# Two attention turns merged: a score bank's read takes over the minimum of the piece in front, and the first stages' order changes

## The reference

```python
u = _rms(h, g_attn_pre)
q_da, k_da, v_da, cq, ckv, kr = jnp.split(u @ w_in, IN_SPLITS, axis=-1)
y_da = _diff_attention(...)   # 4 heads, two components of 64 each, values 128
y_mla = _mla(...)             # 4 heads, 128 + 64 rotary, values 128
h = h + _rms(jnp.concatenate([y_da, y_mla], -1) @ w_o, g_attn_post)
f = jnp.square(jax.nn.relu(_rms(h, g_mlp_pre) @ w_ff1)) @ w_ff2
h = h + _rms(f, g_mlp_post)
```

```python
s1 = (q1 @ k1) * scale + bias     # bias: -slope * distance, or -1e30 where masked
s2 = (q2 @ k2) * scale + bias
a = softmax(s1) - lam * softmax(s2)      # differential attention
p = softmax((q @ k) * scale + bias)      # latent attention, bias 0 or -1e30
```

## Time and profile before

| | |
|---|---|
| device time, median of 3 runs | 2669.18 us (2667.22 to 2671.14) |
| device time of the profiled execution | 2672.47 us |
| its span | 2670.7 us |
| TensorE busy | 2581.2 us, 97% |
| VectorE busy | 1629.5 us, 61% |
| ScalarE busy | 1212.4 us, 45% |
| POOL busy | 326.4 us, 12% |
| granted TensorE clock, mean | 0.99 |

### The profile page before, as it was taken

The page is one execution under the profiler, slowest core; times in us unless marked ns, Lnnn a source line. Parts: engine busy times, 40 slices in busy tenths (PEclk is TensorE's granted clock), DMA queues, the critical chain, the costliest instruction groups (busy, mean ns, idle before and its releaser), DMA issues.

```text
span 2670.7 us, 35310 instructions
## 1 busy us (share of the span) xinstructions
PE 2581.2 (97%) x12220; PEld 2119.1 (79%) x12220; DVE 1629.5 (61%) x3488; ACT 1212.4 (45%) x2177; POOL 326.4 (12%) x303
## 2 busy tenths in 40 slices
PE   8999999899998999999999999999999999999998
PEld 7997687666666888877877888878887887878786
DVE  6213303889996766664457777767767565564665
ACT  6112312577775555554454333533335353443554
POOL 1011001222221222220000000000000001111133
PEclk9999999899999999999999999999999999999999
DMA  6323356724533011016576677656645265666787
GB/s 224 128 102 105 103 166 206 194 62 110 126 133 91 29 37 48 25 51 194 175 243 205 206 240 218 217 168 215 214 135 195 104 225 103 157 171 155 184 174 137
DMA packets 331515, 398.85 MB, mean 149 GB/s; under 512 B 23488, under 2 KB 237744, under 8 KB 323024
## 3 DMA queue, kind: packets, MB, share of 16 engines
q1 hardware_dynamic: 313776, 364.68, 43.6%
q0 software_dynamic: 17568, 31.99, 8.3%
HBM read 240.13 MB, written 156.48 MB: 149 GB/s over the span
## 4 chain that ended last, share of the span: by engine, by line
PE 61%; DVE 3%; ACT 2%; DMA 1%; issue 1%; SPq 1%; POOL 0%; DVEq 0%; ACTq 0%; POOLq 0%
PE ff_ps_x L3143 25%; PE ff_ps_m L3143 13%; PE ff_ps_z L3143 6%; PE ml_ps_s L2026 6%; PE ff_ps_m L1586 4%; PE ml_ps_o L2055 4%; PE ml_ps_t L2039 2%; DMA ml_v_raw<-scr_yT 1%; DVE ff_mv_lo_p L2998 1%; DMA ff_pieces<-scr_acc 0%; PE ff_ps_r L2586 0%; PE mo_ps_t L2603 0%; ACT ff_mv_hi_p L2880 0%; SPq L2213 0%; DVE ff_pieces L2316 0%
## 5 line engine op out<-in xcount | busy, mean ns | idle before, releaser
L3143 PE MATMUL ff_ps_x<-ff_mv_hi_p,ff_st_hi_p 128*128 128x512 f32 x764 | 299.6, 392 | 11.4 <-DVE ff_mv_lo_p L2998 11.4
L3143 PE MATMUL ff_ps_x<-ff_mv_hi_p,ff_st_lo_p 128*128 128x512 f32 x764 | 299.1, 392 | 0.0
L3143 PE MATMUL ff_ps_x<-ff_mv_lo_p,ff_st_hi_p 128*128 128x512 f32 x764 | 298.9, 391 | 0.0
L2026 PE MATMUL ml_ps_s<-wide,ml_qs 128*128 128x416 f32 (+14 forms) x880 | 197.9, 359 | 2.9 <-PEq L137 2.7
L2993 DVE TENSOR_TENSOR ff_st_lo_p<-ff_ps_m,ff_st_hi_p 128x512 fp32r<-128x512 f32 x190 | 130.7, 688 | 104.0 <-ACT ff_st_hi_p L2870 104.0
L2837 POOL DMA_DIRECT2D scr_acc<-ff_pieces x64 | 55.4, 871 | 1030.7 <-DVE ff_pieces L3017 951.4
L3143 PEld LDWEIGHTS ff_ps_x<-ff_mv_hi_p,ff_st_hi_p 128*128 128x128 f32 x764 | 144.3, 189 | 43.5 <-issue 13.6
L2887 ACT ACTIVATE ff_u<-ff_ps_x 128x512 f32<-128x512 f32 x128 | 76.6, 599 | 215.7 <-PE ff_ps_x L3143 215.7
L3143 PEld LDWEIGHTS ff_ps_x<-ff_mv_hi_p,ff_st_lo_p 128*128 128x128 f32 x764 | 144.5, 189 | 30.2
L3143 PEld LDWEIGHTS ff_ps_x<-ff_mv_lo_p,ff_st_hi_p 128*128 128x128 f32 x764 | 144.6, 189 | 29.9
L2026 PEld LDWEIGHTS ml_ps_s<-wide,ml_qs 128*128 128x128 f32 x880 | 152.5, 193 | 18.8 <-issue 7.4
(11 more groups left out here) (298 smaller groups left out, 6375.0 us busy)
## 6 DMA issues: line engine op xcount, KB each, us to landing
st_raw<-in_w_ff SPq DMA_DIRECT2D x64, 512.0 KB, 6.1
scr_hid<-ff_pieces SPq DMA_DIRECT2D x128, 256.0 KB, 2.6
st_raw<-scr_hid SPq DMA_DIRECT2D x64, 512.0 KB, 5.0
ring<-in_w_ff SPq DMA_DIRECT2D x28, 1024.0 KB, 7.8
scr_t<-ring SPq DMA_DIRECT2D x24, 1024.0 KB, 6.4
ring<-scr_t SPq DMA_DIRECT2D x21, 1024.0 KB, 7.9
scr_acc<-ff_pieces POOLq DMA_DIRECT2D x64, 256.0 KB, 4.0
ring<-scr_u SPq DMA_DIRECT2D x13, 1024.0 KB, 8.3
```

What stands on the lines that cost most here:

```text
L2026: m = pe.matmul(ps_s[n % NSB][:, 0:w], q, k, start=j == 0, stop=j == len(pairs) - 1)
L3143: m = pe.matmul(bank[:, :], w[kind][:, k], a[kind][:, k], start=start and k == 0 and i == 0, stop=stop and k == KH - 1 and i == 2, skip_gr ...
```

## The change

Four groups of edits:

1. **First stages.** The second place for a split `cv_proj` weight lies over `in_proj`'s memory in such a way that it is free early; three of the four quarters, in the order 0, 2, 3, 1 (`CV_FIRST`), are split before `in_proj`'s last `high` and `low`, and the first product reads the quarters in that order. At the start the x tiles 4 and 5 are loaded before the second weight tile. POOL's gains in `in_proj` and in the second half of `cv_proj` become eight tensor_scalar operations of one eighth each, and the splits wait for the eighths that they need. SP loads `trig` for tile n + 2 directly behind the latent's store. VectorE's order at the end of the first half of `cv_proj` puts splits ahead of the normalising of the last two tiles.
2. **Both attentions.** The chunk read has scale -scale and takes the minimum, and its starting scalar is the result of the chunk before it (`lowest[..., nth - 1]`) instead of a constant. So `lowest` of the last chunk is the row's. There is no L1448 or L1948 any more; exp waits for `scores_read` of the last chunk and has scale -1. A chunk with a predecessor waits for `scores_read` of it, ahead of the hold.
3. **Memory.** `mx`, `nmax`, `nmax_all` give way to `lowest`.
4. **Squared-ReLU part.** For n = 0 the sum `c11` is added right behind step `p3` instead of behind `p7`.

```diff
             def gain(u):
-                pool.tensor_tensor(w_raw[:, u], w_raw[:, u], g_col[:, :].unsqueeze(2).broadcast_to([P, KD, P]),
-                                   ALU.mult).then_inc(w_gained, 1)
+                for k in range(KD):
+                    pool.tensor_scalar(w_raw[:, u, k], w_raw[:, u, k], g_col[:, k:k + 1], 1.0, ALU.mult, ALU.mult).then_inc(w_gained, 1)
...
             act.wait_ge(cv_gained, 1)
-            act.activation(quarter_of([w_hi], 0), cv_w[:, 0:KD // 4], ACT.Copy).then_inc(shared.w_hi_ready, 1)
+            for q in CV_FIRST[0:3]:
+                act.activation(quarter_of([w_hi, shared.w_hi_second], q), cv_w[:, KD // 4 * q:KD // 4 * (q + 1)], ACT.Copy).then_inc(shared.w_hi_ready, 1)
             high(NM - 1)
...
+CV_FIRST = (0, 2, 3, 1)
...
                 sp.dma_start(scr.latent[r0:r0 + rows, :], cn[0:rows, n % 2, QR:QR + KVR]).then_inc(latent_stored[n % 2], 16)
+                if n + 2 < N:
+                    load_trig(n + 2)
                 sp.wait_ge(lo_ready, n + 1)
                 for src, dst in ((o_hi, scr.c_hi), (o_lo, scr.c_lo)):
                     sp.dma_start(dst[:, :, r0:r0 + rows], f32(src[:, n % 2]).rearrange("p (f t) -> p f t", f=4)[:, :, 0:rows]).then_inc(stored[n % 2], 16)
-                if n + 2 < N:
-                    load_trig(n + 2)
...
             pool.wait_ge(w_loaded, 16 * len(CV_COLS[1]))
-            pool.tensor_tensor(cv_w[:, :, :], cv_w[:, :, :], g_col[:, :].unsqueeze(2).broadcast_to([P, KD, W]), ALU.mult).then_inc(w_gained, 1)
+            for k in range(KD):
+                pool.tensor_scalar(cv_w[:, k], cv_w[:, k], g_col[:, k:k + 1], 1.0, ALU.mult, ALU.mult).then_inc(w_gained, 1)
...
-            for n in range(N - 1):
+            for n in range(N - 2):
                 normalise(n)
                 if n:
                     low(n - 1, pt[(n - 1) % 2])
-            for g in range(NP, 2 * NP - 1):
+            split(NP)
+            normalise(N - 2)
+            for g in (NP + 1, NP + 2):
                 split(g)
+            low(N - 3, pt[(N - 3) % 2])
+            split(2 * NP - 1)
             normalise(N - 1)
-            split(2 * NP - 1)
             low(N - 2, pt[(N - 2) % 2])
             low(N - 1, pt[(N - 1) % 2])
...
             def exp(h, i, c, u, **at):
-                act.wait_ge(max_ready, NT * COMPS * h + COMPS * i + c + 1)
-                act.activation(comp_row(i, c, u), comp_row(i, c, u), ACT.Exp, bias=nmax[:, i % 2, c:c + 1], scale=scale,
+                n = last_chunk[i, c]
+                nth = nth_of(n)
+
+                act.wait_ge(scores_read, NCH * h + n + 1)
+                act.activation(comp_row(i, c, u), comp_row(i, c, u), ACT.Exp, bias=lowest[:, i % 2, c, nth:nth + 1], scale=-1.0,
                                accum_out=total[:, i % 2, c:c + 1]).then_inc(exp_ready, 1)
...
+                if nth:
+
+                    dve.wait_ge(scores_read, NCH * h + n)
 
                 hold(dve, scores_ready, NCH * h + n + 1)
                 dve.tensor_tensor_reduce(out=comp_row(i, c, u)[:, k0:k0 + w], in0=ps_s[n % NSB][:, 0:w],
-                                         in1=bias[u][:, b0:b0 + w], scale=1.0, scalar=LOWEST,
-                                         op0=ALU.add, op1=ALU.max,
-                                         accum_out=mx[:, i % 2, c, nth:nth + 1]).then_inc(scores_read, 1)
-                if k0 + w == META + P * (i + 1):
-                    dve.wait_ge(scores_read, NCH * h + n + 1)
-
-                    dve.tensor_scalar(nmax_all[:, 0:nth + 1], mx[:, i % 2, c, 0:nth + 1], -scale, None, ALU.mult, ALU.min,
-                                      accum_out=nmax[:, i % 2, c:c + 1]).then_inc(max_ready, 1)
+                                         in1=bias[u][:, b0:b0 + w], scale=-scale, scalar=lowest[:, i % 2, c, nth - 1:nth] if nth else -LOWEST,
+                                         op0=ALU.add, op1=ALU.min,
+                                         accum_out=lowest[:, i % 2, c, nth:nth + 1]).then_inc(scores_read, 1)
...
                 then("p3", n)
+                if n == 0:
+                    dve.wait_ge(product_done, done("p2", 0))
+                    add("c11", 0, ps_z, s1, c11_made)
                 hidden("c12", n, c12_made)
```

## The result

The changed kernel takes 2686.48 us (median of 4, 2685.11 to 2688.76), the one before 2669.43 (4 runs): ratio 1.0064, 95% interval 1.0049 to 1.008. It is slower by 17 us; the forecast was 10 slower.

A forecast was written before the change was run, and what follows sets the result against it. TensorE was taken as the bound, VectorE in rows 12 to 15 of each differential-attention head. From the 2669.2 us median, 14.5 us less in front and rest and about 25 more in the differential attention gave 2679 us, range 2655 to 2692.

The forecast's parts named there:

- The price of a dependent chunk: Differential attention: accumulator read 0.085, wait before a hold 0.145, pointer 0.06; 0.29 us when adjacent, 0.21 behind a reciprocal.
- how much reaches the end in rows 8 to 11: Differential attention: VectorE gets +3.4 us a head, mostly in its present pauses, so +1.2 (0.3 to 3) arrives.
- (a): Start: gain cut in 8 lets VectorE in between, x tiles load earlier; 1.5 us less (0 to 2.2).
- (b): First latent product: TensorE's wait for the second weight quarter goes, as three quarters are split earlier; 1.4 us less.
- (c): Latent stage: POOL's long block cut and trig load issued earlier remove TensorE's waits behind o_hi; 7 of 7.2 us.
- (d): Second half of the latent stage: splits ahead of the two last normalises remove two waits; 2.6 us less.
- (e): Squared-ReLU part: moving the c11 add ahead removes TensorE's wait for ScalarE's s1; 1.8 us less.
- (f): Latent attention: dependent chunks cost 0 because VectorE has a third of its time free; last row's chain 0.25 us shorter.
- 1, the cheap wait: Differential attention: wait and nop pass together, a dependent chunk costs 0.18 us; +7, net -7, 2662 us; chance 0.24.
- 2, the free wait: Differential attention: the wait costs nothing, only the pointer's 0.06 us a chunk remains; net -18.5, 2651 us; chance 0.08.
- 4, a front that gives only 6 us: First stages: what is next late refills the holes, so +25 - 6, 2688 us; chance 0.08.
- 3, all of the added work carried through: Differential attention: VectorE's added work arrives in rows 0 to 11 too, +8.3 a head, +33, 2688 us; chance 0.07.

The follow-up runs named there:

- e4: Kernel before, with only a pointer to an older finished maximum as starting scalar of dependent differential-attention chunks, no wait: 2673.54 us, ratio 1.0025.
- the chain alone: Kernel before with only both attention functions replaced by the changed ones: 2700.10 us, ratio 1.012.
- e5: Changed kernel with the hold first in both attentions and the wait on the chunk in front, without a nop, directly at the read: 2659.66 us, ratio 0.9979.
- e3: Kernel before with only the wait on the chunk in front added ahead of the hold in the differential attention: 2712.34 us, ratio 1.0161.
- e1: Changed kernel with both attention functions put back as before: 2648.92 us, ratio 0.9935.
- the mixed version: Changed kernel with attentions as before, except the minimum chained in rows 0 to 7 of the differential attention, wait behind the hold: 2648.99 us, ratio 0.9936.

## Why the prediction came out as it did

- **Sign and mechanism** were right: a dependent chunk waits for its neighbour's result, VectorE is the bound in rows 12 to 15, and the loss there outweighs the gains in front. Expected +25 - 14.5; measured, by the runs of each part, +32 and -17. The chain was forecast 7 too cheap and the gain in front 2.5 too small; that they partly cancel in the total is luck.
- **The price of a dependent chunk** was forecast at 0.29 us and is 0.26 + 0.07 = 0.33. The split into read, wait with nop, and pointer was right term by term (0.085, 0.17 instead of 0.145, 0.067 instead of 0.06). Behind a reciprocal it is about 0.24.
- **The term that was mis-sized** is how much reaches the end in rows 8 to 11: +1.2 us was forecast for a head and +2.6 measured (28.37 against 25.75); in rows 12 to 15 +5.5 forecast, +5.65 measured; in rows 0 to 7 -0.3 forecast and -0.2 measured, all in the third head. The reason is a reading: the first two windows of the earlier trace rows are cut at 670.03, but the first chunk of row 8 is read at 675.74. So "27.85 of 31.46" was no load of rows 8 to 11; it is 23.06 of 25.75 (first windows above), with 2.7 us of idle time, and a demand of 18x0.33 - 8x0.22 = +4.2 can't go into it. The 1.1 us "to spare" in rows 12 to 15 were not slack either: of the 1.7 us that e4 added there, 1.4 arrived.
- **The first head** was taken like the others. It has +10.9 us from row 0 to row 0 of the next (79.3 before, 90.1 after), more than any term says: its rows 8 to 11 take 27.96 us against 23.58, 26.59 with the chain alone. In this head TensorE has 27 us at half clock, against 17 before, which is 5 us of full clock; the rest is open.
- **The clock** was not in the sum. Before, this attention has a granted clock of 1.00 in 508 to 844 us; changed, 0.96 in 516 to 844:

```profile
508.00:844.00 336.00, 323.69 (x1578) 229.01 (x1578) 291.14 (x1091) 237.48 (x411) 70.02 (x56) 1.00 0.41 108
```

```profile
516.00:844.00 328.00, 302.30 (x1393) 208.11 (x1391) 273.72 (x805) 213.89 (x369) 64.36 (x52) 0.96 0.34 92
```

These are five stretches of about 3.4 us at half clock and one of twice that: 24 us, or 12 of full clock not granted. The five start up to 2.5 us behind holes of TensorE of 1.1 to 1.9 us that VectorE's late reads open, such as this one; the long one starts behind a hole of 1.96 us in which TensorE waits for finished rows. One of the five, with the clock of the 2 us behind it:

```profile
645.80 0.59 PE L1536 MATMUL da_ps_s<-da_keys,ahead_q 128*128 128x400 f32 x1 [1.91 <-DVE da_lowest L1463]
...
646.00:648.00 2.00, 2.00 (x5) 1.13 (x5) 1.73 (x6) 0.00 (x0) 1.17 (x1) 0.50 0.03 8
```

By themselves they cost TensorE these 12 us, and the stage less where VectorE is the bound anyway. But with the longest one, at 556 to 564, the second head has its rows 0 to 7 at 34.27 us against 31.23 in the chain alone, which has its full clock in these rows. So VectorE's added time came in part as TensorE working at 1.2 GHz. How much of the loss would be left at full clock no run shows.
- **The front** was forecast at 14.5 and brings 17, with an interval (13 to 22) that holds both. (a) 1.2 us against the profile before, with the VectorE operation of 2.47 us at 0.85, but TensorE's waits behind `u_lo` still 3.5. (b), (c), (d): all waits gone as forecast, 11.2 us by the list and 14.4 by the stage, because waits under a modelled busy time were there too. The profile before was at the slow end in this stage: four later profiles with the same code there take 203 to 205 us, so 9 to 11 us are the gain to expect. (e) 1.3 instead of 1.8. (f) no cost, as forecast.
- **Rivals.** 1, the cheap wait, is refuted for the kernel as it stands (0.26, not 0.12), but e5 shows its price: 6 us under the kernel before where 7 was worked out. It decides at 0.2 us a chunk, as said (e5's chunk costs 0.12 + 0.067 = 0.19); the nop's 0.14 is the whole difference between a slower and a faster kernel. 2, the free wait, fell with e3, and 4, a front that gives only 6 us, with e1. 3, all of the added work carried through, is closest in its number, +33 against +34 for the stage with the chain alone, but by luck: at the measured prices all of VectorE's added work would be 10.3 us a head, 41 in all (46x0.33 + 10x0.24 - 7.1), and eight tenths of it arrive.

## What to carry to other kernels

A reduction that is passed on through an operand costs a round trip between neighbours on the same engine. Put the wait on the result last, directly at the instruction that needs it, and every wait that is kept on a nop before it: the same kernel then goes from 1.0064 to 0.9979 of the time before. Price both sides of such a swap with a kernel that leaves the work out before building it: here the operation to be saved was worth 5 us as measured, and by the estimate above under 10. Of the kernels here that shift exp by the row's own maximum or minimum, the one with the new front and squared-ReLU part and the old attentions is the fastest, 2648.9 us, 0.65% under the kernel before; the mixed version is even with it (2649.0).

## What was not expected of the hardware

- The same hole of TensorE, 2.77 and 2.78 us long at the same step, was followed by a granted clock of 1.00 in one run and of 0.54 for 4 us in another. These two kernels differ in rows 0 to 7; the four with the same attention code show both outcomes too. The up-projection shows what such a stretch costs in itself: it takes 59.8 us with 428 to 436 us at 0.79, and 58.2 us in the runs that have none.
- A latent tile's pace before was 5.97 to 8.96 us with the same instructions, and TensorE's list of waits shows only 11.2 of the 14.4 us that the stage could lose. The distance between the starts of equal steps shows the rest.
- In two of the four heads less work on VectorE gave a fifth of its time back; more work on it took five to nine tenths.
